# In the second half of a two-block fp32 kernel, the rows of the activation tile x lie 1024 instead of 1280 bytes apart, and the eighth without its 64-byte shift

## What is computed

```
first block, 272 tokens (16 meta tokens + 256), from its second layer's query on 256:
  h += gla_mixer(rmsnorm(h))          # q, k, v, r projections, chunked scan, output projection
  h += swiglu(rmsnorm(h))             # 1024 -> 2*2816 -> 1024
  h += dsa_mixer(rmsnorm(h))          # latent attention with a top-k selection
  h += swiglu(rmsnorm(h))             # "ffn1"
second block, 256 tokens:
  h += recurrent_block(rmsnorm(h))    # "lru": 1024 -> 2*1024, conv, gated scan, -> 1024
  h += sqrelu_mlp(rmsnorm(h))         # "mlp0": 1024 -> 4096 -> 1024
  k, v from rmsnorm(h); q from rmsnorm(h); band attention; h += o @ w_o     # "k2", "v2", "q2", "o2"
  h += sqrelu_mlp(rmsnorm(h))         # "mlp1"
```

## Time and profile before

| what | value |
|---|---|
| median of 3 runs | 1182.88 us (1182.33 to 1183.76) |
| profiled execution, its span | 1182.2 us |
| PE busy | 1169.6 us (99%), 9738 matmuls |
| PE weight loads busy | 1140.9 us (97%) |
| DVE busy | 819.2 us (69%) |
| ACT busy | 691.5 us (58%) |
| POOL busy | 89.5 us (8%) |
| read from HBM | 205.66 MB, 175 GB/s over the span |

### The profile page before, as it was taken

The page is one execution under the profiler, slowest core; times in us unless marked ns, Lnnn a source line. Parts: engine busy times, 40 slices in busy tenths (PEclk is TensorE's granted clock), DMA queues, the critical chain, the costliest instruction groups (busy, mean ns, idle before and its releaser), DMA issues. The chain is left out here.

```text
span 1182.2 us, 25988 instructions
## 1 busy us (share of the span) xinstructions
PE 1169.6 (99%) x9738; PEld 1140.9 (97%) x9738; DVE 819.2 (69%) x1296; ACT 691.5 (58%) x1115; POOL 89.5 (8%) x97
## 2 busy tenths in 40 slices
PE   8999999999999999999999999999999999999998
PEld 8999999999998899999999989999999979999998
DVE  7767866665577877666668997675567677776543
ACT  6635765654455567666556976664447576666432
POOL 1000200000110020000120000000013223000000
PEclk9999999999999999999999999999999999999999
DMA  7532655555664336555664556666666424566663
GB/s 270 177 94 89 193 178 177 177 178 192 200 202 144 107 107 190 191 190 193 209 209 155 193 180 192 191 193 191 206 212 205 142 77 153 185 193 193 202 195 106
DMA packets 57577, 207.84 MB, mean 176 GB/s; under 512 B 6352, under 2 KB 7568, under 8 KB 57248
## 3 DMA queue, kind: packets, MB, share of 16 engines
q1 hardware_dynamic: 57136, 203.52, 54.6%
q0 software_dynamic: 288, 3.21, 0.7%
q10 hardware_dynamic: 80, 0.07, 0.0%
HBM read 205.66 MB, written 1.05 MB: 175 GB/s over the span
## 5 line engine op out<-in xcount | busy, mean ns | idle before, releaser
L1679 DVE TENSOR_TENSOR w_lo<-w_raw,w_hi 128x1024 fp32r<-128x1024 f32 x379 | 463.4, 1225 | 68.7 <-ACT w_hi L511 68.1
L511 ACT CAST w_hi<-w_raw 128x1024 fp32r<-128x1024 f32 x379 | 395.1, 1045 | 174.1 <-PE acc L1006 172.2
L1004 PE MATMUL acc<-x_hi,w_hi 128*128 128x256 f32 (+1 forms) x1688 | 479.0, 284 | 2.2 <-DVE w_lo L1679 1.5
L1005 PE MATMUL acc<-x_lo,w_hi 128*128 128x256 f32 (+1 forms) x1688 | 473.3, 280 | 0.0
L1006 PE MATMUL acc<-x_hi,w_lo 128*128 128x256 f32 (+1 forms) x1688 | 473.2, 280 | 0.0
L1004 PEld LDWEIGHTS acc<-x_hi,w_hi 128*128 128x128 f32 x1688 | 317.8, 188 | 6.0 <-DVE x_lo L1699 1.8
L1005 PEld LDWEIGHTS acc<-x_lo,w_hi 128*128 128x128 f32 x1688 | 317.7, 188 | 0.5
L1006 PEld LDWEIGHTS acc<-x_hi,w_lo 128*128 128x128 f32 x1688 | 317.6, 188 | 0.0
L1004 PE MATMUL acc<-m_hi,w_hi 128*128 128x256 f32 x512 | 141.3, 276 | 0.0
L1005 PE MATMUL acc<-m_lo,w_hi 128*128 128x256 f32 x512 | 141.3, 276 | 0.0
L1006 PE MATMUL acc<-m_hi,w_lo 128*128 128x256 f32 x512 | 141.3, 276 | 0.0
(11 more groups left out here) (370 smaller groups left out, 1671.3 us busy)
## 6 DMA issues: line engine op xcount, KB each, us to landing
w_raw<-weights SPq DMA_DIRECT2D x381, 512.0 KB, 4.0
bias<-bias_rows POOLq DMA_DIRECT2D x1, 2048.0 KB, 8.7
h<-hT SPq DMA_DIRECT2D x4, 272.0 KB, 4.5
bias<-bias_rows POOLq DMA_DIRECT2D x1, 1088.0 KB, 8.9
outT<-h SPq DMA_DIRECT2D x4, 256.0 KB, 4.6
con<-constants SPq DMA_DIRECT2D x1, 913.0 KB, 9.3
w_raw<-weights SPq DMA_DIRECT2D x2, 256.0 KB, 3.1
par<-cols SPq DMA_DIRECT2D x1, 84.0 KB, 2.0
```

What stands on the lines that cost most here:

```text
L511: nc.scalar.copy(w_hi[:, slot, :], w_raw[:, slot, :]).then_inc(hi_ready, 1)
L1004: nc.tensor.matmul(out, wh, xh[:, k, tok], start=first and n == 0, stop=False)
L1005: nc.tensor.matmul(out, wh, xl[:, k, tok], start=False, stop=False)
L1679: V.tensor_tensor(w_lo[:, slot, :], w_raw[:, slot, :], w_hi[:, slot, :].bitcast(F32), ALU.subtract)\
```

## The change

`Rows` takes the row step and the shift of the last row as arguments. The views `x_hi`, `x_lo` of the first half keep 320 floats and the shift of 16. The views `xs_hi`, `xs_lo` get a step of `SEQ` = 256 floats (1024 bytes) and no shift, with the same origin. So rows 0 to 7 of xs begin at byte 0, 1024, 2048, ... 7168 of the tile. Before, they began at 0, 1280, 2560, ... 7680, and row 7 at 9024 (8960 + 64). Counted past a multiple of 256, rows 0 to 6 stay at 64, and row 7 goes from 128 to 64. No instruction is added, removed or reordered on any engine; the sizes of the tiles and the addresses of all others stay.

```
 class Rows:
-    def __init__(self, tile, origin=0):
-        self.tile, self.origin = tile, origin
+    def __init__(self, tile, row=ROW, last_shift=LAST_ROW_SHIFT, origin=0):
+        self.tile, self.row, self.last_shift, self.origin = tile, row, last_shift, origin
 
     def __getitem__(self, key):
         p, n, cols = key
-        at = n * ROW + (LAST_ROW_SHIFT if n == KD - 1 else 0) - self.origin
+        at = n * self.row + (self.last_shift if n == KD - 1 else 0) - self.origin
         return self.tile[p, at + cols.start:at + cols.stop]
...
         x_hi, x_lo = Rows(x_hi_rows), Rows(x_lo_rows)
-        xs_hi, xs_lo = Rows(x_hi_rows, META), Rows(x_lo_rows, META)
+        xs_hi, xs_lo = (Rows(tile, SEQ, 0, META) for tile in (x_hi_rows, x_lo_rows))
```

## The result

The changed kernel takes 1194.18 us (median of 6 runs, 1187.47 to 1195.77), the kernel before 1182.91 (6 runs, 1182.33 to 1184.05): ratio 1.0088, 95% interval 1.0071 to 1.0106. The changed kernel's runs spread over 8.3 us, those of before over 1.7. The profiled execution of the changed kernel took 1195.77 us and has a span of 1193.8. The ratios in this document leave out a run that lies more than 1.5% above the fastest of its kernel; there is one, the 1203.33 us of e3.

A forecast was written before the change was run, and what follows sets the result against it. PE (TensorE), busy 99% of the span, was taken as the bound. Savings of 0.88 (ffn1) + 0.64 (mlp0) + 0.64 (mlp1) + 0.12 (k2) + 0.12 (lru) = 2.40 us off 1182.88 gave 1180.5 us, range 1179.5 to 1182.3.

The forecast's parts named there:

- PE bounds the stages on xs: In ffn1 and the first products of mlp0 and mlp1 PE is almost always busy, so matmul savings come off the span.
- The price of row 7's offset: In xs units, row 7 at 128 instead of 64 costs 20 ns; without it a unit takes 2.720 us, not 2.740.
- the forecast 0.64: mlp0's first product: 32 units on xs at 20 ns each, 0.64 us saved.
- The step of 1024 costs nothing: Rows 1024 bytes apart, and the jump back to row 0, cost nothing at offset 64: 2.720 us a unit.
- the slower pace: Late in lru, units take 2.82 to 2.83 us, row 7's shift not showing; never in ffn1, mlp0 or mlp1 stretches.
- rival 3: PE enters the slower pace at a phase's head and keeps it; 56 units in mlp0 and mlp1, +3.6, 1186.5 us; chance 0.03.
- Rival 1: The address is not the cause of the unit's excess and the change does nothing: 1182.9 us; chance 0.08.
- Writers at nothing: ACT and DVE writes to the moved xs rows were costed at nothing; bound 2.4 us either way.
- Lru swallows what PE wins: In lru six units' gain, 0.12 us, comes through; ACT and DVE swallow the other ten, taken as 0, at most 0.20.

The follow-up runs named there:

- e3: Changed kernel, but row 7 of x_lo alone shifted by 64 bytes, to offset 128: 1189.21 us, ratio 1.0050.
- e2: Kernel before with xs rows still 1280 bytes apart, row 7 without its 64-byte shift: 1188.65 us, ratio 1.0063.
- e5: Changed kernel plus three extra matmuls at offset 128 in two units each of ffn1, mlp0 and mlp1: 1183.24 us, ratio 0.9996.
- e1: Changed kernel's xs rows 1024 bytes apart, but row 7 again shifted by 64 bytes: 1182.47 us, ratio 0.9997.
- e6: Kernel before, but in xs row 3 has the 64-byte shift instead of row 7: 1183.01 us, ratio 0.9992.
- e12: Kernel before with first-block attention rows moved 192 bytes and xs row 7 shifted 32 bytes instead of 64, to offset 96: 1200.83 us, ratio 1.0150.
- e4: Changed kernel with all eight rows of xs at a multiple of 256, none at 64: 1198.96 us, ratio 1.0134.

## Why the prediction was wrong

- *PE bounds the stages on xs, and what a matmul gives back or costs comes off or onto the span*: right. ffn1's +3.65 is 42 units x 0.087.
- *The price of row 7's offset is 20 ns a unit, and a unit without it costs 2.720*: right for a fast stretch (mlp0 in the changed kernel, ffn1 in e2, all three in e5). e1 and e2 show that the shift alone makes it, e6 that it does so in another row as well. mlp0's first product gained only 0.25 us of the forecast 0.64, in part because its first two units, which wait for x, took 6.61 us instead of 6.36.
- *The step of 1024 costs nothing*: right (e1).
- **The step that failed** is the one on the slower pace: "it occurs only where ACT and DVE are full or small matmuls lie between, never in the stretches of ffn1, mlp0 and mlp1", and with it that in this pace "row 7's shift does not show". The trace of before has it in ffn1, at 446.84 to 448.96, and its end coincides with row 7. The same is in my: the unit from 671.50 is slow, and the one behind its row 7, from 674.32, is already back. I took the return to 2.740 as PE's own and used it as the evidence against rival 3 ("every one of those long loops went back to 2.740 after the wait at its head"). It went back because of the very thing that the change removes. So I counted the shift as a cost alone, and gave the case that its loss makes the kernel slower 0.03.
- *Rival 3* was the right mechanism, with its size too small: 0.107 a unit and the loss of the gain were right (0.087 on x), but I put only 56 units on xs in danger, those in the loops of mlp0 and mlp1. ffn1, which I left out, cost 3.65 us, and a slow stretch drags the following product on m or mid with it, which is 5.7 of the 11.6 us. Both MLP loops at once, as I had it, is in neither profile of the changed kernel.
- *Rival 1* was wrong: the place of the operand does matter: 113.3 (64), 118.7 (0), 120.0 (128) ns, and the time did not stay at 1182.9. The rule of the Trainium skill that the prediction cites for it (page "TensorE: Matmul & The Clock Gate", section "Wait — 56ns, not 53.3ns?"), one distance for a width, does not hold for these fp32r products.
- *Writers at nothing*: the page's DVE and ACT sums are unchanged (819.2; 691.3 against 691.5). Right.
- *Lru swallows what PE wins*: it swallowed what PE lost, too: +0.2 us, with nine of its sixteen units on x in the slow pace.

What is shown: that the shift, and not the step, holds the time; that matmuls at offset 128 end the slow pace, and the same matmuls at 64 do not; that one such group sometimes fails; that in e12 a row at 96 leads from the fast pace into the slow one. What stays open: what the two paces are inside TensorE, why the offset of one row moves PE from one to the other, and what decides at a phase's head which pace PE comes out with. In the two profiles of the changed kernel it was the same for ffn1 and not for mlp1, and in e2, which has no shifted row either, ffn1 was fast.

## What to carry to other kernels

When a piece of layout costs a little in every unit and seems to do nothing, look for the places in the trace where the machine is out of step and see what ends them, before it is removed: the first units after a wait tell more than the forty steady ones after them. Compare starts with starts in a stream of equal matmuls, and put the moving operand's rows where the distance is smallest (of the offsets seen here, 64 bytes past a multiple of 256), but measure whole kernels: all rows at 64 lost 11 us here, and one row of eight at 128 kept the time even. When a kernel's runs spread over 8 us and its sibling's over 2, look for a state that is entered by chance; the median says little about the change until it is found. A narrow spread does not rule it out: e12's runs lie within 2.9 us, and its profile is slow in all long stretches.

## What the runs showed of the hardware that I had not expected

- A stream of LDWEIGHTS and 256-column fp32r matmuls at clock 1.00 runs at 113.3 or 117.8 ns a matmul, with the same operands, for 80 us and more without changing over, and over a change of the moving tile.
- The offset of the moving rows changes the price: 113.3 ns at 64, 118.7 at 0 (e4), 120.0 at 128 past a multiple of 256, all with stationary tiles at 128, the only place that they had. One row of three matmuls at 128 among rows at 64 costs 20 ns; x_lo alone at 128 costs 27 (e3).
- Three matmuls in a row at 128 end the slow pace, sometimes only at the second try (five of nine nudges worked); x_lo alone did not in 28 units of e3's mlp1 and did once in its lru. A row at 96 turned the fast pace into the slow one five times of five (e12); in the profiled execution all long stretches are slow, and the other three runs take as long.
